# Feed-forward up projection: each pair of weight slots as seven block products of a one-level Strassen scheme

## The reference

```
def conv_glu_ffn(h, w_up, conv_w, conv_b, w_down):
    up = h @ w_up                                   # 1024 x 5632
    a, b = up[..., :D_FF], up[..., D_FF:]
    a_pad = jnp.pad(a, ((0, 0), (CONV_W - 1, 0), (0, 0)))
    c = (a_pad[:, 0:seq_len] * conv_w[0] + a_pad[:, 1:seq_len + 1] * conv_w[1]
         + a_pad[:, 2:seq_len + 2] * conv_w[2] + conv_b)
    return (jax.nn.gelu(c) * b) @ w_down
...
h = h + conv_glu_ffn(rmsnorm(h, norm2_g[l]), w_up[l], conv_w[l], conv_b[l], w_down[l])
```

## Time and profile before

| | us |
|---|---|
| median of 3 runs (1738.45 to 1740.54) | 1739.4 |
| the profiled execution, its own time | 1738.78 |
| its span | 1737.0 |
| TensorE busy | 1664.0 |
| VectorE busy | 617.1 |
| ScalarE busy | 420.2 |
| of it the up projection: matmuls of L633, busy | 305.5 |
| down projection: matmuls of L644, busy | 151.3 |

### The profile page before, as it was taken

One profiled execution on the slowest core, in us unless ns is written; L12 is line 12 of the kernel. 1 busy time (PEld: TensorE's weight loads), 2 busy tenths in 40 slices (PEclk: granted clock), 3 DMA queues, 4 the chain that ended last, 5 costly groups with the idle time before them and its releaser, 6 DMA issues.

```text
span 1737.0 us, 15417 instructions
## 1 busy us (share of the span) xinstructions
PE 1664.0 (96%) x6188; PEld 1000.4 (58%) x6188; DVE 617.1 (36%) x1021; ACT 420.2 (24%) x801; POOL 116.7 (7%) x82
## 2 busy tenths in 40 slices
PE   7999999999999999999999999999998998999996
PEld 6884777778876666665444334555533434555542
DVE  8537343322022112112000118665501318665402
ACT  3643544420010000001000222233222222143321
POOL 4023000000000000000000050000000050001001
PEclk9999999999999999999999999999999999999998
DMA  5211111222212222222222111111121211111121
GB/s 199 73 37 49 49 49 49 98 88 67 78 49 75 83 73 75 83 73 73 73 84 73 49 48 61 37 49 48 62 61 48 61 37 61 49 43 44 37 73 49
DMA packets 31656, 111.56 MB, mean 64 GB/s; under 512 B 3520, under 2 KB 3776, under 8 KB 31072
## 3 DMA queue, kind: packets, MB, share of 16 engines
q1 hardware_dynamic: 31248, 108.32, 19.8%
q0 software_dynamic: 336, 2.23, 0.4%
HBM read 108.45 MB, written 2.10 MB: 64 GB/s over the span
## 4 chain that ended last, share of the span: by engine, by line
PE 90%; DVE 6%; ACT 2%; issue 1%; ACTq 1%; DMA 0%; POOL 0%; DVEq 0%; SPq 0%
PE PS L688 20%; PE PS L633 18%; PE PS L644 9%; PE PS L1034 6%; PE PS L483 6%; PE PS L383 5%; PE PS L602 3%; PE PS L615 3%; PE PS L459 2%; DVE SC L1950 2%; PE PS L780 2%; PE PS L585 1%; PE PS L363 1%; PE PS L737 1%; PE PS L716 1%; PE PS L753 1%
## 5 line engine op out<-in xcount | busy, mean ns | idle before, releaser
L688 PE MATMUL PS<-HN,ring 128*128 128x512 f32 x896 | 406.4, 603 | 4.9 <-DVE HN L1653 4.9
L633 PE MATMUL PS<-HN,ring 128*128 128x257 f32 (+1 forms) x1056 | 305.5, 453 | 2.4 <-DVE HN L1653 2.4
L688 PEld LDWEIGHTS PS<-HN,ring 128*128 128x128 f32 x896 | 168.4, 193 | 203.5 <-issue 199.3
L633 PEld LDWEIGHTS PS<-HN,ring 128*128 128x128 f32 x1056 | 201.5, 191 | 106.0 <-issue 86.5
L644 PE MATMUL PS<-PJ,ring 128*128 128x512 f32 x352 | 151.3, 592 | 1.0 <-DVEq L1637 1.0
L644 PEld LDWEIGHTS PS<-PJ,ring 128*128 128x128 f32 x352 | 66.8, 190 | 85.6 <-issue 83.7
L1034 PE MATMUL PS<-PJ,ring 128*128 128x512 f32 x256 | 112.1, 592 | 0.0
L483 PE MATMUL PS<-HN,ring 128*128 128x264 f32 x448 | 107.0, 393 | 2.2 <-ACT PJ L1178 2.2
L383 PE MATMUL PS<-HN,ring 128*128 128x264 f32 x448 | 103.2, 391 | 2.5 <-DVE HN L1653 2.5
L383 PEld LDWEIGHTS PS<-HN,ring 128*128 128x128 f32 x448 | 85.7, 192 | 18.4 <-issue 2.9
L483 PEld LDWEIGHTS PS<-HN,ring 128*128 128x128 f32 x448 | 84.2, 193 | 19.6 <-issue 3.7
(11 more groups left out here) (399 smaller groups left out, 1784.6 us busy)
## 6 DMA issues: line engine op xcount, KB each, us to landing
ring<-wst SPq DMA_DIRECT2D x188, 512.0 KB, 3.6
X<-xT SPq DMA_DIRECT2D x16, 264.0 KB, 5.3
V<-small POOLq DMA_DIRECT2D x2, 1024.0 KB, 5.1
outT<-X SPq DMA_DIRECT2D x8, 256.0 KB, 2.1
consts<-cst SPq DMA_DIRECT2D x1, 1291.5 KB, 13.6
V<-s5w SPq DMA_DIRECT2D x1, 1280.0 KB, 10.5
POS<-pos SPq DMA_DIRECT2D x1, 256.0 KB, 13.8
params<-par SPq DMA_DIRECT2D x1, 209.5 KB, 2.6
```

What stands on the lines that cost most here:

```text
L633: ins = mm(dst, ring[:, s, b * P:b * P + P], src, start=(b == 0), stop=(b == KD - 1))
L688: ins = mm(bank(b), ring[:, r, i * P:i * P + P], HN[:, i, 0:SEQ], start=(i == 0), stop=(i == KD - 1))
```

## The change

Two neighbouring slots, block i of `a` and block i of `b`, are taken as one 2 x 2 block matrix: rows are `a` and `b` features, columns are the two halves of the input (chunks 0 to 3, `a11` and `a21`; chunks 4 to 7, `a12` and `a22`). The activations are a 2 x 2 block matrix too: the halves of the input by the halves of the tokens (257 each, of 514). The product of the two takes eight block products before. Now it takes seven (Winograd's form of Strassen's scheme), each of four matmuls of 257 columns: `product` in TensorE's program. Four sums of weight halves are needed for each block (`sums`, into `SA`, two buffers), four sums of activation halves once (`TB`), and seven sums of products for each block, which VectorE makes from PSUM and from two products that ScalarE copies to SBUF (`kept`, into `SN`).

The order on VectorE: `sums(0)` stands before the norm; the activation sums behind it; then for each block j the two halves of the convolution's input, the convolution, `sums(j + 1)`, the sums for `b` (into `BV`), and the product with the gelu (`times`). On ScalarE the gelu of block i-1 comes between the copies of products 0 and 3 of block i. On TensorE products go round the eight banks, and the seven products have a wait for their bank each; `sa_ready` is waited for before product 2. Slots are freed in twos, at the first and the second matmul of the next block.

```diff
+FF0 = 12 + 4 + 16 + 2 + 8 + 8
...
+        SA = cut(2 * 4 * 512, 2, 4, 512)
+        TB = cut(4 * 4 * 257, 4, 4, 257)
+        at[0] = 13374
+        SN = cut(2 * 2 * 257, 2, 2, 257)
+        UU = cut(2 * 257, 2, 257)
+        BV = cut(512)
...
-            for i in range(NFF // 2):
-                for k in range(WSLOTS):
-                    s = (2 + k) % 4
-                    slot(s)
-                    put(k)
-                    for h in range(2 if k % 2 == 0 else 1):
-                        for b in range(KD):
-                            dst = PS[k][:, h, 0:257] if k % 2 == 0 else PS[k][:, 0, :]
-                            src = HN[:, b, 14 + 257 * h:271 + 257 * h] if k % 2 == 0 else HN[:, b, NMETA:T]
-                            if k == 0 and h == 0:
-                                chunk_in(b)
-                            ins = mm(dst, ring[:, s, b * P:b * P + P], src, start=(b == 0), stop=(b == KD - 1))
-                            if h == 0 and b == 0:
-                                freed(ins, (s - 1) % 4)
-                    ins.then_inc(SEMS[f"act_full{k}" if k % 2 == 0 else f"dve_full{k}"], 1)
+            def product(i, x, left, right, b0=None):
+                at = 7 * i + x
+                bnk = at % 8
+                if i == 0:
+                    if x % 2 == 0:
+                        put(x // 2, False)
+                if at >= 8:
+                    old, y = divmod(at - 8, 7)
+                    if y in (0, 3):
+                        pe.wait_ge(SEMS["snap"], 2 * old + (1 if y == 0 else 2))
+                    else:
+                        pe.wait_ge(SEMS["ff_u"], 5 * old + (0, 1, 2, 0, 3, 4, 5)[y])
+                for b in range(4):
+                    if i == 0 and b0 is not None:
+                        chunk_in(b0 + b)
+                    ins = mm(PS[bnk // 2][:, bnk % 2, 0:257], left[:, b * P:b * P + P], right[:, b, :], start=(b == 0), stop=(b == 3))
+                    if x == 0 and b < 2 and (i or b == 0):
+                        freed(ins, (FF0 + 2 * i - 1 - b) % WSLOTS)
+                ins.then_inc(SEMS["ff_p"], 1)
+            lo = [HN[:, 0:4, 14 + 257 * h:271 + 257 * h] for h in range(2)]
+            hi = [HN[:, 4:8, 14 + 257 * h:271 + 257 * h] for h in range(2)]
+            for i in range(NFF):
+                sa, sv = (FF0 + 2 * i) % WSLOTS, (FF0 + 2 * i + 1) % WSLOTS
+                slot(sa)
+                slot(sv)
+                product(i, 0, ring[:, sa, 0:512], lo[0], 0)
+                product(i, 1, ring[:, sa, 512:1024], hi[0], 4)
+                pe.wait_ge(*n("sa_ready"))
+                if i == 0:
+                    pe.wait_ge(*n("tb_ready"))
+                product(i, 2, SA[:, i % 2, 1], TB[:, 1])
+                product(i, 3, SA[:, i % 2, 0], TB[:, 0])
+                product(i, 4, SA[:, i % 2, 3], hi[1])
+                if i == 0:
+                    pe.wait_ge(*n("tb_ready", 2))
+                product(i, 5, SA[:, i % 2, 2], TB[:, 2])
+                product(i, 6, ring[:, sv, 512:1024], TB[:, 3])
             pe.wait_ge(*n("hid_done"))
             for p in range(4):
                 put(p)
@@ -642,8 +673,8 @@
                 slot(s)
                 for m in range(KD):
                     ins = mm(PS[m // 2][:, m % 2, :], ring[:, s, m * P:m * P + P], hid[:, k, :], start=start, stop=stop)
-                    if m == 0:
-                        freed(ins, (s - 1) % 4)
+                    if m == 0 or (start and m == 1):
+                        freed(ins, (s - 1 - m) % 4)
...
-            for i in range(NFF // 2):
-                for m in range(2):
-                    act.wait_ge(*n(f"act_full{2 * m}"))
-                    af(FA[:, :].rearrange("p (a b) -> p a b", a=2), PS[2 * m][:, :, 0:257], ACT.Copy).then_inc(SEMS["ffa"], 1)
-                    act.wait_ge(*n("ffc"))
-                    af(GL[:, :], CV[:, :], ACT.Gelu_apprx_tanh).then_inc(SEMS["ffg"], 1)
+            def gelu():
+                act.wait_ge(*n("ffc"))
+                af(GL[:, :], CV[:, :], ACT.Gelu_apprx_tanh).then_inc(SEMS["ffg"], 1)
+            def kept(i, x):
+                at = 7 * i + x
+                act.wait_ge(SEMS["ff_p"], at + 1)
+                af(SN[:, i % 2, x // 3], PS[at % 8 // 2][:, at % 2, 0:257], ACT.Copy).then_inc(SEMS["snap"], 1)
+            for i in range(NFF):
+                kept(i, 0)
+                if i:
+                    gelu()
+                kept(i, 3)
+            gelu()
...
+            def sums(j):
+                sa, sv = (FF0 + 2 * j) % WSLOTS, (FF0 + 2 * j + 1) % WSLOTS
+                for k in (FF0 + 2 * j, FF0 + 2 * j + 1):
+                    dve.wait_ge(SEMS[f"w_ready{k % WSLOTS}"], 16 * (k // WSLOTS + 1))
+                a11, a12 = ring[:, sa, 0:512], ring[:, sa, 512:1024]
+                a21, a22 = ring[:, sv, 0:512], ring[:, sv, 512:1024]
+                s1, s2, s3, s4 = (SA[:, j % 2, k] for k in range(4))
+                tt(s3, a11, a21, ALU.subtract)
+                link(tt(s1, a21, a22, ALU.add))
+                link(tt(s2, s1, a11, ALU.subtract))
+                link(tt(s4, a12, s2, ALU.subtract))
+                post("sa_ready")
+            def times(j):
+                dve.wait_ge(*n("ffg"))
+                link(tt(hid[:, j, :], GL[:, :], BV[:, :], ALU.mult))
+            sums(0)
             norm(X[:, :, :], lambda k: v1("g2", k), T)
-            for i in range(NFF // 2):
-                for m in range(2):
-                    def col(name):
-                        return par1[:, bass.ds(i * 2 + (m + V1[name][0]), 1)]
-                    dve.wait_ge(*n("ffa"))
-                    link(ts(CV[:, :], FA[:, 2:514], col("cw2"), col("cb"), ALU.mult, ALU.add))
-                    link(stt(CV[:, :], FA[:, 1:513], col("cw1"), CV[:, :], ALU.mult, ALU.add))
-                    stt(CV[:, :], FA[:, 0:512], col("cw0"), CV[:, :], ALU.mult, ALU.add).then_inc(SEMS["ffc"], 1)
-                    mark(f"free{2 * m}")
-                    dve.wait_ge(*n("ffg"))
-                    dve.wait_ge(*n(f"dve_full{2 * m + 1}"))
-                    tt(hid[:, i * 2 + m, :], GL[:, :], PS[2 * m + 1][:, 0, :], ALU.mult).then_inc(SEMS[f"free{2 * m + 1}"], 1)
-                    join()
+            lo = [HN[:, 0:4, 14 + 257 * h:271 + 257 * h] for h in range(2)]
+            hi = [HN[:, 4:8, 14 + 257 * h:271 + 257 * h] for h in range(2)]
+            join()
+            link(tt(TB[:, 0], lo[1], lo[0], ALU.subtract))
+            link(tt(TB[:, 1], hi[1], TB[:, 0], ALU.subtract))
+            post("tb_ready")
+            tt(TB[:, 2], hi[1], lo[1], ALU.subtract).then_inc(SEMS["tb_ready"], 1)
+            tt(TB[:, 3], hi[0], TB[:, 1], ALU.subtract).then_inc(SEMS["tb_ready"], 1)
+            for j in range(NFF):
+                def part(x):
+                    at = 7 * j + x
+                    dve.wait_ge(SEMS["ff_p"], at + 1)
+                    return PS[at % 8 // 2][:, at % 2, 0:257]
+                def col(name):
+                    return v1(name, j)
+                s1, s5, u2, u3 = SN[:, j % 2, 0], SN[:, j % 2, 1], UU[:, 0], UU[:, 1]
+                dve.wait_ge(*n("snap"))
+                tt(FA[:, 0:257], s1, part(1), ALU.add).then_inc(SEMS["ff_u"], 1)
+                tt(u2, s1, part(2), ALU.add).then_inc(SEMS["ff_u"], 1)
+                join()
+                dve.wait_ge(*n("snap"))
+                link(tt(u3, u2, s5, ALU.add))
+                tt(FA[:, 257:514], u3, part(4), ALU.add).then_inc(SEMS["ff_u"], 1)
+                join()
+                link(ts(CV[:, :], FA[:, 2:514], col("cw2"), col("cb"), ALU.mult, ALU.add))
+                link(stt(CV[:, :], FA[:, 1:513], col("cw1"), CV[:, :], ALU.mult, ALU.add))
+                link(stt(CV[:, :], FA[:, 0:512], col("cw0"), CV[:, :], ALU.mult, ALU.add))
+                post("ffc")
+                if j + 1 < NFF:
+                    sums(j + 1)
+                tt(u3, u2, part(5), ALU.add).then_inc(SEMS["ff_u"], 1)
+                join()
+                link(tt(BV[:, 255:512], u3, s5, ALU.add))
+                tt(BV[:, 0:255], u3[:, 2:257], part(6)[:, 2:257], ALU.add).then_inc(SEMS["ff_u"], 1)
+                join()
+                times(j)
             post("hid_done")
```

More of the change, by code:

```diff
@@ L128, in build @@
                      "b_zero", "c_act", "c_dve", "c_in", "c_mul", "c_tok", "d_kr", "d_misc", "d_mul", "d_tok", "d_tr", "g_used",
-                     "par2_in", "w2_free", "x1_ready", "x2_e", "x2_o", "y_done", "g_free0", "g_free1"):
+                     "par2_in", "w2_free", "x1_ready", "x2_e", "x2_o", "y_done", "sa_ready", "tb_ready", "snap", "ff_p", "ff_u", "g_free0", "g_free1"):
             sem(name)
```

## The result

The changed kernel takes 1707.2 us (median of four runs, 1706.7 to 1707.5) against 1739.7 (four runs too): a ratio of 0.9816, interval 0.9803 to 0.9829. The forecast was 1705.8. The profiled execution has a span of 1705.7 us, 31.3 less than before.

What follows compares the result with a forecast made beforehand. TensorE, busy 96% of the span, was taken as the bound. From 1737.0 us, - 35.1 for blocks, + 0.6 start, + 0.9 end gave 1703.4; with 1.8 and 0.6 for execution and median, 1705.8 us, range 1702.2 to 1716.

Steps and rivals of the forecast that it cites:

- Price by columns: TensorE, up projection: matmuls cost by columns, 216.6 ns per 257, so 13.80 us per block becomes 12.13, 35.1 us saved.
- The chain of the weight sums: VectorE from product 4 to the next block's product 2: 6.2 us against TensorE's 6.93, slack 0.7, no stall.
- unseen waits: VectorE's four extra waits per block, two for weights, two for banks: from nothing to 0.3 us, still fitting.
- The start: Block 0: TensorE stands 2.3 us for the activation differences; 0.6 us lost.
- half clock at the norm: TensorE starts block 0 at 497.93 and runs at 1.2 GHz until about 501.4.
- a fall like the one at 498 costs 1.7: A clock fall to 1.2 GHz behind a new gap lasts 3.4 us and costs 1.7.
- The first rival: Clock falls at the new gaps, start and end: one gives 1707.5 us, both 1709.2; chance 0.20.
- The end: Before the down projection TensorE resumes 2.1 us after its last matmul, where it was 1.2; 0.9 us lost.
- The clock rival: Clock falls to 1.2 GHz at the new start and end gaps: 1707.5 us with one, 1709.2 with both; chance 0.20.
- VectorE a little late: Chain and waits exceed 6.93 us, so TensorE waits for weight sums in each block: 1710 to 1717 us; chance 0.15.
- VectorE slow: Weight sums with both inputs in SBUF run at 1635 ns, as beside GpSimd: 1769 us; chance 0.03.
- Waits of TensorE: Each product's bank wait costs up to 0.05 us, 7.7 us in all: 1713.5 us; chance 0.06.

Runs made afterwards that it cites:

- Experiment 3: Changed kernel with an eighth product in each block (product 6 made twice): 1745.9 us, ratio 1.0042 to the kernel before.
- experiment 2: Changed kernel with one more weight sum before TensorE's post in blocks 1 to 21: 1707.4 us; with three more: 1738.0 us.
- experiment 5: Changed kernel again: 1707.1 us; product 4 earlier in block 0: 1706.3; down projection's first slot waiting bank by bank: 1700.9, again 1701.5; both edits: 1701.2, again 1701.8.
- second profile: Changed kernel run again unaltered, on the chip of the gap edits: 1707.1 us, with no clock fall behind the start's gap.

## Why the prediction was right, point by point

- **Price by columns.** Right. 12.13 us per block was forecast and 12.15 measured; the seven waits cost 0.02 us per block together, against an upper bound of 0.35. Experiment 3 shows it from the other side.
- **The chain of the weight sums.** Right, slack 0.7 forecast, 0.81 read and 0.80 measured by experiment 2. Every step had its row: 0.69 for 0.70, 0.42 for 0.42, 0.55 + 0.75 + 0.75 as before. From VectorE's start behind product 4 (511.35) to the end of the last sum (516.99) it took 5.64 us, forecast 5.68; of the unseen waits only those for the weights show, 0.21 in place of 0.04 before the first sum.
- **The start.** The path over VectorE was right: product 2 was forecast 7.5 us behind the first matmul (505.4 against 497.93) and came after 7.4. The term was set at 0.6 us. It came at 2.3 in one profile, and in the other, without a fall, at 0.6 (498.06 to 514.22, 16.16 us against 15.56). What failed is the clock's part: no fall was charged behind the new gap, where one cost 1.7 us in the first profile. The half clock at the norm, which the working carried over from the earlier trace rows, changes nothing, as experiment 5 shows; nor does "a fall like the one at 498 costs 1.7" hold for that place. The first rival, with one fall, had 1707.5.
- **The end.** 0.9 us forecast, 0.9 measured; experiment 5 shows that it lay on the path.
- **Outside the stage** I had nothing, and it holds -1.2 and +1.5 us. No step of mine covered falls of the clock that come elsewhere in the new execution: one fewer ahead, one more behind, and that the two nearly cancel is luck. The clock rival's reason for few falls, the 1.00 behind the gap before 966.98, was true of that trace and not of the two of the changed kernel, which fall at 934 us.
- **The number.** In spans the forecast was 1703.4, and 1705.7 came, 2.3 us more: 1.7 for the fall in block 0, 0.4 for the 21 blocks, 0.2 outside. The medians hide 0.9 of it, for the forecast added 0.6 for the median of before, and the profiled execution after lies 0.3 above its own. In the second profile the stretch was within 0.4 us of the forecast (459.5 - 33.6 = 425.9, measured 426.3). So the account of the stage was right, and part of the closeness of the whole was luck.
- **Rivals.** VectorE a little late: not here, and from 0.8 us on it would have been. VectorE slow: shown to be possible with GpSimd at work. Waits of TensorE: no.

## What to carry to other kernels

When TensorE is busy all the time and its matmuls are priced by columns, saving one product in eight by sums on an idle engine is worth nearly the columns of that product (1.74 us, of which 1.65 of 13.8 came in each block), as long as the sums keep their distance: read the slack from the end of the last sum to the first weight load that uses it, and multiply whatever goes beyond it by the number of blocks. A new dependence costs mostly at the two ends of a stage; look there for work that doesn't depend on it (product 4 in block 0, banks already free in the down projection). Compare edits of a few microseconds over their own stretch of the trace, for the whole time moves by as much through falls of the clock elsewhere. And look at what a shifted stage now lies beside: a delay can push VectorE's work next to GpSimd's.

## What the runs showed of the hardware that I had not expected

- The same gap of 2.0 us, in the same kernel, was followed by 3.4 us at 1.2 GHz in one execution and by none in another; after gaps of 2.36 us both were seen too (0.52 in the earlier trace rows, 1.00 in the changed kernel). A fall costs 1.7 us in dense work (275.1 against 273.4) and nothing where TensorE waits for the norm. The Trainium skill, TensorE: Matmul & The Clock Gate, Part 1, has the activity that counts looked at in windows that run free of the kernel; one gap with and without a fall agrees with it, though no run here moves a gap and nothing else.
- An edit worth 2.2 us in its stretch gained 6 in most executions, those with a mean granted clock of 0.986 to 0.988 in place of 0.982.
- GpSimd's additions slow not only VectorE's sums of two SBUF tensors (0.69 to 1.63 us) but also its `tensor_scalar` with one (0.55 to as much as 1.31 us). A delay of 1.6 us that put the first norm beside them made it 8.10 us in place of 5.52.
